# Layer 2 of a transformer and RWKV kernel: the bonus product reads from PSUM, key norms come first, SiLUs in two panels, root and spreads sooner

## The reference, cut to what matters

```
proj = h @ w_in                      # r, k, v, conv input, z_rwkv, z_conv
a    = sigmoid(a0 + (xa @ a1) @ a2)
kk   = heads(k * kk_scale)
kk   = kk / max(sqrt(sum(kk * kk)), 1e-12)          # key norm, per head
k    = k * (1.0 + (a - 1.0) * ka_scale)
y    = wkv7(r, decay, k, v, -kk, kk * a)
bonus = sum(r * k * r_k) * v                        # per head
c    = silu(layer_norm(conv(...)))                  # goes into c @ w_conv_out
```

## Time and profile before

| what | value |
|---|---|
| median of 3 runs | 2310.91 us (2307.06 to 2311.28) |
| the profiled execution's own time | 2307.39 us |
| its span | 2305.4 us |
| mean granted TensorE clock | 0.986 of full speed |
| PE busy | 2210.0 us, 96% |
| DVE, ACT, POOL busy | 1033.4, 881.2, 1025.0 us |

### The profile page before, as it was taken

The page is one execution under the profiler, slowest core; times in us unless marked ns, Lnnn a source line. Parts: engine busy times, 40 slices in busy tenths (PEclk is TensorE's granted clock), DMA queues, the critical chain, the costliest instruction groups (busy, mean ns, idle before and its releaser), DMA issues.

```text
span 2305.4 us, 35770 instructions
## 1 busy us (share of the span) xinstructions
PE 2210.0 (96%) x14532; PEld 1820.9 (79%) x14532; DVE 1033.4 (45%) x1643; ACT 881.2 (38%) x1494; POOL 1025.0 (44%) x607
## 2 busy tenths in 40 slices
PE   7999999999999999999998999997888899999998
PEld 6867888888987687888887788876777678888888
DVE  5254622221337635222114798866784555222112
ACT  5265533322322745332224323273445535333222
POOL 4423544444554145444436344444440555444543
PEclk9999999999999999999999999998999999999999
DMA  6610243333353022333333333342401422333332
GB/s 177 148 29 29 81 122 98 99 93 96 90 125 92 2 65 76 98 101 92 103 89 118 97 93 100 103 154 83 147 31 40 163 76 83 104 98 99 93 95 70
DMA packets 387156, 216.13 MB, mean 94 GB/s; under 512 B 37023, under 2 KB 378759, under 8 KB 386483
## 3 DMA queue, kind: packets, MB, share of 16 engines
q1 hardware_dynamic: 383587, 201.93, 31.0%
q0 software_dynamic: 2736, 10.75, 1.2%
q10 hardware_dynamic: 672, 1.18, 0.1%
HBM read 199.80 MB, written 15.56 MB: 93 GB/s over the span
## 4 chain that ended last, share of the span: by engine, by line
PE 87%; DVE 4%; ACT 3%; POOL 2%; issue 2%; DMA 0%; ACTq 0%; POOLq 0%; DVEq 0%
PE ps L2478 25%; PE ps L2480 25%; PE ps L2479 25%; PE ps L2688 2%; PE ps L2663 2%; PE ps L2673 2%; POOL x_res L938 1%; PE ps L2651 1%; POOL w_lo L871 1%; ACT w_hi L1068 1%; PE ps L2846 0%; DVE tmpf L2146 0%; PE ps L2955 0%; PE ps L2551 0%; PE ps L2995 0%
## 5 line engine op out<-in xcount | busy, mean ns | idle before, releaser
L871 POOL TENSOR_TENSOR w_lo<-raw,w_hi 128x1024 fp32r<-128x1024 f32 (+2 forms) x344 | 822.9, 2396 | 888.9 <-ACT w_hi L1068 884.0
L2478 PE MATMUL ps<-h_hi,w_hi 128*128 128x512 f32 (+1 forms) x2048 | 789.4, 385 | 16.9 <-DVE h_lo L1783 4.8
L2479 PE MATMUL ps<-h_hi,w_lo 128*128 128x512 f32 (+1 forms) x2048 | 778.1, 380 | 0.0
L2480 PE MATMUL ps<-h_lo,w_hi 128*128 128x512 f32 (+1 forms) x2048 | 778.0, 380 | 0.0
L1068 ACT ACTIVATE w_hi<-raw 128x1024 fp32r<-128x1024 f32 (+1 forms) x344 | 358.2, 1042 | 1091.0 <-PE ps L2480 1075.6
L2478 PEld LDWEIGHTS ps<-h_hi,w_hi 128*128 128x128 f32 x2048 | 385.9, 188 | 103.8 <-issue 24.0
L2480 PEld LDWEIGHTS ps<-h_lo,w_hi 128*128 128x128 f32 x2048 | 385.9, 188 | 73.6
L2479 PEld LDWEIGHTS ps<-h_hi,w_lo 128*128 128x128 f32 x2048 | 386.5, 189 | 72.4 <-issue 1.2
L2478 PE MATMUL ps<-hid_hi,w_hi 128*128 128x512 f32 (+1 forms) x616 | 221.8, 360 | 0.0
L2480 PE MATMUL ps<-hid_lo,w_hi 128*128 128x512 f32 (+1 forms) x616 | 220.9, 359 | 0.0
L2479 PE MATMUL ps<-hid_hi,w_lo 128*128 128x512 f32 (+1 forms) x616 | 220.9, 359 | 0.0
(11 more groups left out here) (363 smaller groups left out, 2570.5 us busy)
## 6 DMA issues: line engine op xcount, KB each, us to landing
raw<-in_w_gu SPq DMA_DIRECT2D x88, 512.0 KB, 3.9
raw<-in_w_in SPq DMA_DIRECT2D x56, 512.0 KB, 3.8
raw<-in_w_down SPq DMA_DIRECT2D x32, 448.0 KB, 3.8
raw<-in_ffn_w_gate SPq DMA_DIRECT2D x22, 512.0 KB, 3.8
raw<-in_ffn_w_up SPq DMA_DIRECT2D x22, 512.0 KB, 3.8
raw<-in_w_in_b SPq DMA_DIRECT2D x20, 512.0 KB, 3.8
raw<-in_w_down SPq DMA_DIRECT2D x16, 512.0 KB, 3.9
raw<-in_w_out SPq DMA_DIRECT2D x16, 512.0 KB, 4.0
```

Source lines behind the costliest of these rows:

```text
L871: nc.gpsimd.tensor_tensor(lo[:, k0:, :], src[:, k0:, :], hi[:, k0:, :].bitcast(f32), ALU.subtract).then_inc(lo_done, 1)
L2478: nc.tensor.matmul(bank, wh[:, k, :], ah[:, part], start=first, stop=False)
L2479: nc.tensor.matmul(bank, wl[:, k, :], ah[:, part], start=False, stop=False)
L2480: return nc.tensor.matmul(bank, wh[:, k, :], al[:, part], start=False, stop=end)
```

## The change

`mix_of` now makes two PSUM tiles for each chunk: the factor of the keys as before, and r*r_k (a copy with a scale). They rotate through three banks (4, 5, 6), so that both of DVE's products read one operand from PSUM. The products go to seven SBUF tiles, no longer four. `kk_of` is done for all eight chunks before the first `rk_of`. The SiLUs stand in slots 6 and 7 (four each), no longer in 6, 7 and 8; the root in slot 7, no longer 8; `kk_hi` in slot 8, no longer 9; `mix_of` in slots 11 to 13 (3, 3, 2 chunks), no longer 10 to 13 (2 each). On PE the spreads stand inside and behind groups 10 and 11, no longer inside 10 to 13; the bonus sums behind groups 13 and 14, no longer 12 and 14.

```diff
+        def rk_buffer(m):
+
+            return starts[:, :] if RK_BUFFERS[m] == "starts" else tmp_flat[RK_BUFFERS[m]]
...
-        k_mix = [ps[:, 4, :], starts[:, :]]
+        MIX_BANKS = (4, 5, 6)
+        RK_BUFFERS = (0, 1, 2, 3, 8, 9, "starts", 0)
...
+        MIX_SLOTS = {11: (0, 1, 2), 12: (3, 4, 5), 13: (6, 7)}
         EXP_SLOTS = {14: (0, 1), 15: (2, 3), 16: (4, 5), 17: (6, 7)}
         LAB_SLOT = 3
-        SILU_SLOTS = {6: range(3), 7: range(3, 6), 8: range(6, KD)}
+        SILU_SLOTS = {6: range(4), 7: range(4, KD)}
...
             def b_of(m):
                 c = HEAD_ORDER[m]
-                pool.wait_ge(sg["rk_ready"], m + 1)
+                pool.wait_ge(sg["kk_ready"], m + 1)
+                pool.wait_ge(sg["k_mix"], 2 * m + 1)
...
                 if m == 0:
                     act.wait_ge(sg["rows_lo"], 1)
-                    act.wait_ge(sg["cum_ready"], KD)
                     act.wait_ge(sg["a_ready"], KD)
-                if m >= 2:
-                    act.wait_ge(sg["rk_ready"], m - 1)
-                nc.scalar.activation(k_mix[m % 2], u_b[:, c, :], ACT.Identity, scale=vec("k_a_2", c), bias=omu[:, 3, c:c + 1]
+                if m == 1:
+                    act.wait_ge(sg["kk_ready"], KD)
+                if 2 * m >= 3:
+                    act.wait_ge(sg["rk_step"], 2 * m - 2)
+                nc.scalar.activation(ps[:, MIX_BANKS[2 * m % 3], :], u_b[:, c, :], ACT.Identity, scale=vec("k_a_2", c),
+                                     bias=omu[:, 3, c:c + 1]).then_inc(sg["k_mix"], 1)
+                if m == 0:
+                    act.wait_ge(sg["kk_ready"], KD)
+                if 2 * m + 1 >= 3:
+                    act.wait_ge(sg["rk_step"], 2 * m - 1)
+                nc.scalar.activation(ps[:, MIX_BANKS[(2 * m + 1) % 3], :], u_r[:, c, :], ACT.Copy, scale=vec("r_k_2", c)
                                      ).then_inc(sg["k_mix"], 1)
...
-                if i == KS - 1:
+                if i == max(SILU_SLOTS):
                     kk_root()
-                if i == KS:
+                if i == max(SILU_SLOTS) + 1:
                     act.wait_ge(sg["kk_rec"], 1)
                     rows_high(kk_hi[:, :], ps[:, 4, :], -1.0)
-                p = i - KS - 1
-                if 0 <= p < NP:
-                    mix_of(2 * p)
-                    mix_of(2 * p + 1)
+                for m in MIX_SLOTS.get(i, ()):
+                    mix_of(m)
...
-                dve.wait_ge(sg["k_mix"], m + 1)
-                link(nc.vector.tensor_tensor(u_k[:, c, :], u_k[:, c, :], k_mix[m % 2], ALU.mult))
-                if m >= 4:
+                dve.wait_ge(sg["k_mix"], 2 * m + 1)
+                nc.vector.tensor_tensor(u_k[:, c, :], u_k[:, c, :], ps[:, MIX_BANKS[2 * m % 3], :], ALU.mult
+                                        ).then_inc(sg["rk_step"], 1)
+                dve.wait_ge(sg["k_mix"], 2 * m + 2)
+                dve.wait_ge(sg["rk_step"], 2 * m + 1)
+                if RK_BUFFERS.index(RK_BUFFERS[m]) < m:
                     dve.wait_ge(sg["rk_sums"], 1)
-                nc.vector.scalar_tensor_tensor(tmp_flat[m % 4], u_r[:, c, :], vec("r_k_2", c), u_k[:, c, :], ALU.mult, ALU.mult
-                                               ).then_inc(sg["rk_ready"], 1)
+                nc.vector.tensor_tensor(rk_buffer(m), u_k[:, c, :], ps[:, MIX_BANKS[(2 * m + 1) % 3], :], ALU.mult
+                                        ).then_inc(sg["rk_step"], 1)
...
-            for p in range(NP):
-                kk_of(2 * p)
-                kk_of(2 * p + 1)
-                rk_of(2 * p)
-                rk_of(2 * p + 1)
+            for m in range(KD):
+                kk_of(m)
+            for m in range(KD):
+                rk_of(m)
...
-                pe.wait_ge(sg["rk_ready"], 4 * four + 4)
-                head_sums(7, four, lambda m: tmp_flat[m % 4]).then_inc(sg["rk_sums"], 1)
+                pe.wait_ge(sg["rk_step"], 8 * four + 8)
+                head_sums(7, four, rk_buffer).then_inc(sg["rk_sums"], 1)
...
-                if i in (KS + 3, KS + 5):
-                    rk_sums((i - KS - 3) // 2)
+                if i in (10, 11):
+                    kk_spread(4 * i - 38)
+                    kk_spread(4 * i - 37)
+                if i in (13, 14):
+                    rk_sums(i - 13)
...
-                p = i - KS - 1
-                if 0 <= p < NP:
-                    kk_spread(2 * p)
-                    kk_spread(2 * p + 1)
+                if i in (10, 11):
+                    kk_spread(4 * i - 40)
+                    kk_spread(4 * i - 39)
```

More of the change, by code:

```diff
@@ L2896, in inside @@
                     pre_a_and_w(2 * (i - 3) + 1)
-                p = i - KS - 1
-                if 0 <= p < NP:
-                    kk_spread(2 * p)
-                    kk_spread(2 * p + 1)
+                if i in (10, 11):
+                    kk_spread(4 * i - 40)
+                    kk_spread(4 * i - 39)
             project("z", between={i: (lambda i=i: beside(i)) for i in range(2 * KD)},
-                    within={i: (lambda i=i: inside(i)) for i in range(3, KS + 1 + NP)})
+                    within={i: (lambda i=i: inside(i)) for i in range(3, 12)})
             def tokens(j, cb):
```

## The result

The changed kernel takes 2285.57 us (median of 4 runs, 2285.22 to 2286.24) where the kernel before takes 2310.34 in the runs beside it (2307.06 to 2311.28): ratio 0.9896, 95% interval 0.9878 to 0.9913. A second comparison (the fifth experiment) gave 2285.43 against 2309.77, ratio 0.9894, interval 0.9878 to 0.991. 2286.5 was forecast, in a range from 2281.5 to 2293.5.

The account below looks back on a forecast made before the run. PE, busy 96% of the span, bounds the kernel through its waits and clock. 24.5 us back less 2.0 lost nets 22.5: 2284.9 from the profiled time, 2288.4 from the median; forecast 2286.5 between them, range 2281.5 to 2293.5.

Parts of the forecast that it names:

- The three holes: PE waits before the first spread and both bonus sums, 4.19, 6.98 and 7.69 us start to start; all forecast to close.
- z: Part holding the change, measured from first square sums to PE's wait on z_stage; net saving forecast 22.5 us.
- the two holes: PE's waits at the bonus sums: 6.98 + 1.44 and 7.69 + 1.70 + 0.14 us back, with low clock behind them.
- The loss before the second square sums: In slot 6 a SiLU and a high part precede the squares, so PE's second kk_sums start 1.23 us later.
- The loss before group 10: Panel 10's high part waits for ACT, its low part comes late to PE: 0.8 us lost, bounds 0 and 2.25.
- The first spread: PE may spread at 1567.77 but arrives at 1569.7, so the first hole closes: 4.19 and 2.35 us back.
- The first bonus sums: PE wants their first four chunks at the end of group 13, 1592.4; DVE is through by 1590.9, slack 1.5.
- The clock rival: New waits before kk_sums and group 10 bring PE's lower clock back: 2.35 us more, 2288.9; chance 0.2.
- The rival of thin slack: Low parts of panels 13 to 16 late behind b_of, or steps cost 0.9: +4 us, 2290.5; chance 0.1.
- The rival of a held product with a PSUM operand: POOL holds such DVE products after all; late holes (17.95) stay, net 4.5 at most, 2304.4; chance 0.04.
- slow hand-overs: 16 ACT-DVE steps through three banks, each as long as a held product's 4.88: slower, 2347; chance 0.03.
- Everything from there on moves as a block: Behind z nothing changes: decays wait on the last bonus sums before group 15, so later work only shifts earlier.

Follow-up runs that it names:

- the fifth experiment: The changed kernel run again unaltered, beside the kernel before: 2285.43 us against 2309.77, ratio 0.9894.
- experiment 2: Changed kernel with the early part undone (SiLUs in three slots, root in slot 8, high part in slot 9), bonus part kept: 2292.77 us, ratio 0.993.
- experiment 1: Changed kernel with DVE's bonus product reading r from SBUF again, ACT's copies made but unused: 2294.55 us, ratio 0.9944.
- Experiment 3: Changed kernel with the last two squares ahead of the SiLUs in slot 6: 2289.66 us, ratio 0.9914.
- experiment 6: Kernel before with only the early part (SiLUs in slots 6 and 7, root in 7, kk_hi in 8): 2305.71 us, ratio 0.9984.

## Why the prediction was right

**The three holes closed.** The first by the early root: experiment 2 moves it back and the wait of 4.07 and the clock of 0.53 are there again. Late ones: the second SBUF input beside a working POOL is what held the products, as the prediction had it; experiment 1 puts the bonus product's back and 8.55 us of z with it. The late part is worth 17.95 in all (z 115.67 with the bonus part alone). Its other 9.4 comes from what experiment 1 leaves changed, and no run splits it: the order (norms first, mixes ahead of the products), more buffers, and the key product that no longer reads `starts`. The prediction gave the two holes 17.95 together and did not split them.

**The loss before the second square sums** was put at 1.23 and is 8.81 - 7.59 = 1.22 (from the first square sums to the second, after and before); its idle time, put at 1.4, is 1.23.

**The loss before group 10** was put at 0.8 and is 22.38 - 20.47 - 1.22 = 0.69 (from the first square sums to group 10, after and before).

**The first spread** was placed 1.9 after it may start, at 1569.7; shifted by the 2.20 of this execution it started at 1569.63. The first bonus sums were placed at 1592.4 and came, shifted in the same way, at 1592.61; the second at 1599.7 and came at 1600.12; group 15 at 1601.6 and came at 1601.97.

**The clock rival** did not come true, 1.00 behind both waits, in all three profiles. Experiment 3 shows that it was not idle: with one wait of 2.16 in place of two the clock was 0.66.

**The rival of thin slack** did not come true either, and in iteration 12 it was less near than the prediction has it. Panel 14's low part ended at 1590.01 and the bonus sums stand ahead of group 14, which started at 1592.26: a slack of 2.25. The 0.3 of the prediction left out the 1.85 of these sums.

**The rival of a held product with a PSUM operand and that of slow hand-overs** are excluded by products of 0.69 beside POOL and steps of 0.66 and 0.70.

**The Trainium skill's rule** in "SBUF — State Buffer", section "Who interferes with whom", names who contends rightly: two SBUF inputs beside a GpSimd instruction that reads SBUF, and not one. Its size, read as the prediction did, as one whole instruction of the winner, is too small here: the loser was held over 3 of POOL's instructions (4.83) and over 10, with a DMA issue between them (15.00). The measurement decides.

**"Everything from there on moves as a block"** holds within what the profiles can tell: the stretch behind z scatters by 2.7 us between executions of the same kernel. It was stated more firmly than one profile allows.

**The size.** z gave 22.4 of the 22.5. The medians differ by 24.8 and 24.3; their intervals, 20 to 28 us, hold 22.5. The three profiled executions of each kernel differ by 20.9 in the mean of their own times, so no profile shows where 2 more would lie. Against profiled executions alone the forecast was 2284.9; against the median it would have been 2288.4. The choice between the two was the part that was not worked out, and it happened to land 0.9 from the result.

## What to carry to other kernels

Before counting a DVE instruction's time, look at what POOL does beside it. If it reads two tensors from SBUF, it ended here with POOL's unbroken run of work, plus 0.55 us (128x512) or 1.08 (128x1024); put one operand in PSUM, or let POOL wait for the product where it is due, since a DMA issue in the run is no break. Closing a hole by moving work earlier left smaller waits at the next places; here two of 1.2 and 0.5 cost 1.9, and one of 2.2 cost 3.8 with the low clock behind it, which such a wait does not bring every time. And profile the kernel before more than once before explaining a difference of two microseconds in a part that the change does not touch.

## What the hardware showed that was not expected

- A DVE product of 0.75 us lasted 15.00 beside POOL's run of ten products and a DMA issue of 0.58, ending 0.56 behind the run. In experiment 1 it ended 0.55 behind, and the 1024-element one of `wk_tri` 1.08 behind, with 8.93 and with 3.48. The issue of 0.58 in the run did not let DVE in.
- A DVE product need not start behind POOL's instruction to be held. In the kernel before, the product shown started 0.35 ahead of the low part, while POOL was still at a DMA issue (1592.80 to 1593.38), and ended 0.57 behind POOL's next product (1596.95). Why it did not go first is open.

```profile
1593.05 4.47 DVE L2146 SCALAR_TENSOR_TENSOR tmpf<-u_rkk,vecs,u_k 128x512 f32<-128x512 f32 x1
```
```profile
1593.40 2.35 POOL L871 TENSOR_TENSOR w_lo<-raw,w_hi 128x1024 fp32r<-128x1024 f32 x1
1595.69 1.26 POOL L969 TENSOR_TENSOR u_b<-u_b,u_rkk 128x512 f32<-128x512 f32 x1
```

- POOL did not slow down in return: its low part took 2.42 beside a held product and 2.41 beside products that read PSUM.
- The same wait of PE costs more or less as the low clock falls: behind the two late holes 0.70 and 0.61 in the kernel before, 0.50 and 0.50 in the kernel of experiment 6, with the same brackets. 1.56 us of a gain of 4.53 went that way.
